# A fused two-block transformer kernel: the mixed 512 and 256-column form for more chunks of its feed-forward stages

## The chip, the core and the metric

The kernel runs on one core of a Trainium2 chip. The metric is the device time of one execution in microseconds (us). Each instruction belongs to an engine with its own in-order queue: TensorE (PE, with its weight loads shown as PEld), VectorE (DVE), ScalarE (ACT), GpSimd (POOL) and SyncE (SP), which here issues nearly all DMAs. Engines wait for each other through counting semaphores.

## The reference, cut to what matters

Two transformer blocks are applied to x of 256 rows and 1024 columns in float32. Four feed-forward layers (D_FF = 2816) take most of the work; the kernel calls them F0, F1, F2, F3. Between them lie a mixing layer with two kinds of attention (M1) and one with a Fourier part and latent attention (M2).

```
def swiglu(x, w_gate, w_up, w_down):
    return (jax.nn.silu(x @ w_gate) * (x @ w_up)) @ w_down

def first_block(...):
    mods = (jax.nn.silu(c) @ w_ada[l] + b_ada[l]).reshape(B, N_MOD, D_MODEL)
    n = modulate(rmsnorm(h, g_pre[l, 0]), shift(0), scale(0))
    f = swiglu(n, w_ffn_gate[l, 0], w_ffn_up[l, 0], w_ffn_down[l, 0])     # F0
    h = h + 0.5 * gate(0) * rmsnorm(f, g_post[l, 0])
    ...                                                                  # M1, F1

def second_block(...):
    mod = c_act @ ada_w[l] + ada_b[l]
    x = x + 0.5 * g1[:, None, :] * swiglu_2(h, ...)                      # F2
    ...                                                                  # M2, F3
```

The products `silu(c) @ w_ada` and `c_act @ ada_w` (1024 by 9216 each) are not done as matmuls of the stages. They are spread as work of DVE over the feed-forward stages, most of it in F0.

## The kernel before

**Precision.** Every float32 matrix is split into a high part and a low part in the type fp32r: ACT copies the raw weights to `w_hi` (`split_hi`, L816) and DVE subtracts to get `w_lo` (`split_lo`, L1201). A product is then three matmuls: hi by hi, hi by lo and lo by hi.

**A feed-forward stage** is cut into 11 chunks (NC) of 256 columns of D_FF. For a chunk c, PE makes the gate and the up product (`gate_up_half`, first half and second half of the 1024 rows of the weights, one 1 MB slot of weights each), then ACT takes Silu of the gate part and DVE multiplies it by the up part into `h_act`. While that goes on, PE does the down product of chunk c - 1 (`downs`), which needs `hT_hi` (ACT) and `hT_lo` (DVE, L1294) of that chunk. So one pass of `body` on PE is: wait for the product of chunk c - 1 (`h_ready`), gate and up of c, down of c - 1. The pass of `body` on DVE that belongs to it has the split of the down weights, `hT_lo`, the conditioning updates `ada`, the split of the next chunk's first half of gate and up weights, the product, and the split of the second half.

**Two forms of the gate and up product.** In the narrow form (`col_group`, L1929, L1931, L1932) all three matmuls of a block of 128 outputs have 256 columns, 96 matmuls per chunk. Four blocks share two PSUM banks; the product is one Silu on ACT and one multiplication on DVE (L1317). In the mixed form the high weights meet the high and the low part of the input side by side in one matmul of 512 columns (L1948), and the low weights meet the high part in one of 256 (L1954), so a chunk has 32 of 512 columns and 32 of 256. Each block then fills a bank of its own (banks 0 to 3), and what stands in the right half of a bank has to be added to the left half. That is an ACT copy, a DVE addition (L1307), the Silu on ACT (L897), an ACT copy and a DVE addition (L1309), and then the multiplication (L1312). `wide(f, c)` says which chunks take the mixed form: before, chunks 2 to 9 of F1, F2 and F3, none of F0. Chunk 0 of each stage is computed in rows (t = 0 and 1 are the two halves of the 256 rows) in banks 0 and 1, and is turned by transposes (`row_transposes`) in bank 0.

**The conditioning updates.** `ada(f, half, j)` (L1280 for j = 0, L1283 otherwise) adds row block j of the conditioning weights, times silu(c), to an accumulator; j runs from 0 to 7, one per chunk, in chunks 1 to 8. Each has one buffer in `arena` for each half, so the load of block j waits for the update with block j - 1. In F0 both halves have 3072 columns (1.5 MB each), in F1 1024 and 3072, in F2 3072 and 2048, in F3 1024 and none.

**What sets the order.** Each engine's order is written out by hand, with a hardware loop over the middle chunks. In `body` on DVE the place of the first update depends on the form:

```
if mods and wide(f, c):
    ada(f, 0, c - 1)
split_lo(*down_piece(f, c - 1))
...
if mods:
    if not wide(f, c):
        ada(f, 0, c - 1)
```

SP issues for each chunk, in this order: the down weights, the two conditioning loads, the two halves of the gate and up weights; each waits for the buffer that it fills.

Of the kernel before, what the change touches and what calls it, by code (L numbers as in the profile page):

```python
# [9 lines left out]
ALU = mybir.AluOpType  # L10
# [35 lines left out]
def program(nc, a, out):  # L46

    ctx = ExitStack()
    with ctx:
# [384 lines left out]

        def wide(f, c):

            return f != "F0" and (not isinstance(c, int) or 1 < c < NC - 1)

        def wide_at(f, c):

            return c + ((NC - 3) * (FFN.index(f) - 1) - 1)

        def down_piece(f, c):
            if isinstance(c, int) and c == NC - 1:
# [370 lines left out]
        def _(act):  # L815
# [63 lines left out]
            def body(f, c, extra=None):  # L879

                i = FFN.index(f) * NC
                split_hi(*down_piece(f, c - 1))
                if isinstance(c, int) and c == 1:
                    act.wait_ge(row_tr, FFN.index(f) + 1)
                    copy(hT_hi[:].rearrange("p j n -> p (j n)"), ps[:, 0, :]).then_inc(ht_hi, 1)
                else:
                    act.wait_ge(h_ready, c + i)
                    copy(hT_hi[:], h_act[:]).then_inc(ht_hi, 1)
                if extra:
                    split_hi(*extra)  # L890
                split_hi(*(down_piece(f, c) if isinstance(c, int) and c == NC - 1 else gate_up(f, 0, c + 1)))
                if wide(f, c):
                    act.wait_ge(gate_mm, wide_at(f, c))
                    act.wait_ge(h_ready, c + i)
                    copy(sil[:], ps[:, 0:2, S:2 * S]).then_inc(g_rest, 1)
                    act.wait_ge(g_sum, wide_at(f, c))
                    act.activation(sil[:], sil[:], ACT.Silu).then_inc(silu_done, 1)  # L897
                    used(act, gate_up(f, 1, c))
                    act.wait_ge(ht_lo, c + h_parts(f))
                    copy(h_act[:], ps[:, 2:4, S:2 * S]).then_inc(u_rest, 1)  # L900
                else:
                    used(act, gate_up(f, 1, c))
                    wait(act, h_ready, c + i)
                    b = 2 if isinstance(c, int) and c == 1 else 0
                    act.activation(sil[:], ps[:, b, :].rearrange("p (k n) -> p k n", n=S), ACT.Silu).then_inc(silu_done, 1)
                if not (isinstance(c, int) and c == NC - 1):
                    split_hi(*gate_up(f, 1, c + 1))

            def row_silu_out(f):

                i = FFN.index(f)
                act.wait_ge(row_mm, STAGES.index(f) + 1)
                act.activation(sil[:, 0, :], ps[:, 0, 0:FC], ACT.Silu).then_inc(row_silu, 1)
                used(act, gate_up(f, 1, 0))
                act.activation(sil[:, 1, :], ps[:, 1, 0:FC], ACT.Silu).then_inc(silu_done, 1)

            def ffn(f, next_e=None, next_b=None, n=PIECE):

# [3 lines left out]
                body(f, 1)  # L922
                if f == "F0":
                    used(act, down_piece(f, 0))
                with act.Fori(2, NC - 1) as c:
                    body(f, c)
                body(f, NC - 1, extra=next_e and (*next_e, n))
                act.wait_ge(h_ready, NC * (FFN.index(f) + 1))
# [261 lines left out]
        def _(dve):  # L1190
# [95 lines left out]
            def body(f, c, mods=False, hook=None, extra=None):  # L1286
# [3 lines left out]
                    ada(f, 0, c - 1)  # L1290
                split_lo(*down_piece(f, c - 1))
                dve.wait_ge(ht_hi, c + h_parts(f))
                h = ps[:, 0, :].rearrange("p (j n) -> p j n", n=S) if isinstance(c, int) and c == 1 else h_act[:]
                dve.tensor_tensor(hT_lo[:], h, hT_hi[:].bitcast(F32), ALU.subtract).then_inc(ht_lo, 1)  # L1294
                if mods:
                    if not wide(f, c):
# [579 lines left out]
        def _(pe):  # L1876
# [89 lines left out]
            def body(f, c, mid=None, first=None):  # L1966
                i = FFN.index(f) * NC
                if not (isinstance(c, int) and c <= 1):
                    pe.wait_ge(h_ready, c + i)
                if first:  # L1970
                    first()
                gate_up_half(f, 0, c)
                if mid:
                    mid()
                gate_up_half(f, 1, c)
                if isinstance(c, int) and c == NC - 1:
                    return
                downs(f, c)
# [590 lines left out]
```

## Time and profile before

| | |
|---|---|
| time, median of 3 runs | 1097.07 us (1097.07 to 1097.42) |
| profiled execution, its own time | 1097.06 us |
| its span in the trace | 1095.3 us |
| PE busy | 1066.7 us, 97% of the span |
| DVE busy | 848.7 us, 77% |
| ACT busy | 546.6 us, 50% |
| POOL busy | 50.3 us, 5% |
| chain that ended last | PE 88%, DVE 4%, ACT 2%, DMA 2% |

The span is that of the instructions of the traced execution; the time of the execution is 1.8 us longer. The chain that ended last is followed back from the last instruction, at each step to what released it. Busy shares are means over the whole kernel, and the stages differ: what a change is worth in one stage has to be read from the rows of that stage.

### The profile page before, as it was taken

The numbers are of one execution on the slowest core, as the hardware profiler recorded it, in microseconds if no ns is written. First come the engines' busy times: TensorE is split into PE (matmuls) and PEld (weight loads), VectorE is DVE, ScalarE is ACT, GpSimd is POOL, SyncE is SP. The second block draws the span as 40 slices with busy tenths as digits, with TensorE's granted clock in tenths as the row PEclk, the third lists the DMA queues.
The fourth block names the chain that finished last, engine by engine and source line by source line (L and its number), as shares of the span: only waits on it lengthen the run. The fifth ranks groups of instructions, "written<-read, shape, count | busy, mean of one in ns | idle before, by whom it ended". The sixth has DMA issues, their size and how long they took to land.

```text
span 1095.3 us, 16473 instructions
## 1 busy us (share of the span) xinstructions
PE 1066.7 (97%) x6295; PEld 939.1 (86%) x6295; DVE 848.7 (77%) x908; ACT 546.6 (50%) x658; POOL 50.3 (5%) x78
## 2 busy tenths in 40 slices
PE   3999999999999999999999999999999999999997
PEld 2999999889988788888988888898888878888886
DVE  6899888678887788888778998867875787666665
ACT  4444343564765644544564444455645356444452
POOL 1000000101221100000010000000100000000001
PEclk9999999999999999999999999999999999999999
DMA  9999997557424598997569999744562546766651
GB/s 340 381 402 390 388 396 262 171 118 230 134 78 154 192 337 312 321 313 239 187 243 383 344 352 355 250 145 135 185 223 78 175 133 216 229 213 232 220 177 58
DMA packets 147141, 265.28 MB, mean 242 GB/s; under 512 B 9769, under 2 KB 104470, under 8 KB 141974
## 3 DMA queue, kind: packets, MB, share of 16 engines
q1 hardware_dynamic: 145376, 261.30, 69.0%
q0 software_dynamic: 1056, 3.17, 1.0%
q8 instruction: 31, 0.51, 0.2%
q10 hardware_dynamic: 662, 0.16, 0.1%
q14 instruction: 16, 0.13, 0.0%
HBM read 263.34 MB, written 1.27 MB: 242 GB/s over the span
## 4 chain that ended last, share of the span: by engine, by line
PE 88%; DVE 4%; ACT 2%; DMA 2%; issue 2%; SPq 1%; POOL 1%; POOLq 0%; DVEq 0%; ACTq 0%
PE ps L1948 16%; PE ps L1879 12%; PE ps L1880 12%; PE ps L1881 12%; PE ps L1954 8%; PE ps L1929 7%; PE ps L1932 7%; PE ps L1931 7%; DMA w_raw<-in_w_ffn_up 1%; DMA arena<-in_w_ada 1%; ACT w_hi L816 1%; DVE w_lo L1201 1%; DVE y_row L1362 1%; SPq L631 1%; PE ps L1899 1%
## 5 line engine op out<-in xcount | busy, mean ns | idle before, releaser
L1201 DVE TENSOR_TENSOR w_lo<-w_raw,w_hi 128x2048 fp32r<-128x2048 f32 (+2 forms) x169 | 380.4, 2255 | 110.0 <-ACT w_hi L816 109.1
L816 ACT ACTIVATE w_hi<-w_raw 128x2048 fp32r<-128x2048 f32 (+2 forms) x169 | 317.5, 1883 | 261.1 <-PE ps L1881 112.1
L1929 PE MATMUL ps<-nT_both,w_hi 128*128 128x256 f32 x672 | 191.7, 285 | 0.0
L1932 PE MATMUL ps<-nT_both,w_lo 128*128 128x256 f32 x672 | 190.1, 283 | 0.0
L1931 PE MATMUL ps<-nT_both,w_hi 128*128 128x256 f32 x672 | 190.1, 283 | 0.0
L1948 PE MATMUL ps<-nT_both,w_hi 128*128 128x512 f32 x768 | 187.1, 391 | 0.0
L1948 PEld LDWEIGHTS ps<-nT_both,w_hi 128*128 128x128 f32 x768 | 141.1, 188 | 27.3
L1929 PEld LDWEIGHTS ps<-nT_both,w_hi 128*128 128x128 f32 x672 | 128.8, 192 | 0.9
L1283 DVE SCALAR_TENSOR_TENSOR arena<-arena,c_act 128x3072 f32<-128x3072 f32 (+2 forms) x49 | 129.4, 2650 | 0.0
L1931 PEld LDWEIGHTS ps<-nT_both,w_hi 128*128 128x128 f32 x672 | 128.9, 192 | 0.5
L1932 PEld LDWEIGHTS ps<-nT_both,w_lo 128*128 128x128 f32 x672 | 128.8, 192 | 0.0
L1879 PE MATMUL ps<-w_hi,hT_hi 128*128 128x512 f32 x320 | 125.0, 391 | 0.0
L1880 PE MATMUL ps<-w_lo,hT_hi 128*128 128x512 f32 x320 | 125.0, 391 | 0.0
L1881 PE MATMUL ps<-w_hi,hT_lo 128*128 128x512 f32 x320 | 124.5, 389 | 0.0
L1954 PEld LDWEIGHTS ps<-nT_both,w_lo 128*128 128x128 f32 x768 | 101.6, 191 | 5.6
L1954 PE MATMUL ps<-nT_both,w_lo 128*128 128x256 f32 x768 | 103.4, 282 | 0.0
L1879 PE MATMUL ps<-w_hi,nT_both 128*128 128x512 f32 (+2 forms) x256 | 99.9, 390 | 0.5 <-DVE nT_both L1221 0.3
L1881 PE MATMUL ps<-w_hi,nT_both 128*128 128x512 f32 (+2 forms) x256 | 97.5, 381 | 0.0
L1880 PE MATMUL ps<-w_lo,nT_both 128*128 128x512 f32 (+2 forms) x256 | 97.4, 380 | 0.0
L1881 PEld LDWEIGHTS ps<-w_hi,hT_lo 128*128 128x128 f32 x320 | 60.1, 188 | 12.8
L1879 PEld LDWEIGHTS ps<-w_hi,hT_hi 128*128 128x128 f32 x320 | 60.2, 188 | 11.5
L1880 PEld LDWEIGHTS ps<-w_lo,hT_hi 128*128 128x128 f32 x320 | 60.2, 188 | 11.0
(299 smaller groups left out, 1218.7 us busy)
## 6 DMA issues: line engine op xcount, KB each, us to landing
arena<-in_w_ada SPq DMA_DIRECT2D x16, 1536.0 KB, 9.5
arena<-in_ada_w SPq DMA_DIRECT2D x16, 1536.0 KB, 8.3
w_raw<-in_w_in SPq DMA_DIRECT2D x44, 512.0 KB, 4.6
w_raw<-in_ffn_w_down SPq DMA_DIRECT2D x44, 512.0 KB, 4.1
w_raw<-in_w_ffn_gate SPq DMA_DIRECT2D x42, 512.0 KB, 7.0
w_raw<-in_w_ffn_up SPq DMA_DIRECT2D x42, 512.0 KB, 8.2
w_raw<-in_w_ffn_down SPq DMA_DIRECT2D x42, 512.0 KB, 4.7
w_raw<-in_ffn_w_gate SPq DMA_DIRECT2D x42, 512.0 KB, 4.1
```

The lines of the kernel that those rows point to most:

```text
L631: sp.dma_start(dst, cols).then_inc(first_loaded[j], 16)
L816: copy = lambda o, i: act.activation(o, i, ACT.Copy)
L1201: dve.tensor_tensor(lo(s, n), raw(s, n), hi(s, n).bitcast(F32), ALU.subtract).then_inc(lo_ready[s], 1)
L1283: dve.scalar_tensor_tensor(acc, ada_raw[:, half, 0:n], c_act[:, blk, bass.ds(j, 1)], acc, ALU.mult, ALU.add)\
L1879: pe.matmul(o, xh, wh, start=start, stop=False, skip_group_check=True)
L1880: pe.matmul(o, xh, wl, start=False, stop=False, skip_group_check=True)
L1881: return pe.matmul(o, xl, wh, start=False, stop=stop, skip_group_check=True)
L1929: pe.matmul(o, hi(s)[:, cols], nT_hi[:, kk, :], start=(half == first_half and k == 0 and i % 2 == 0), stop=False, skip_group_check=True)
L1931: pe.matmul(o, hi(s)[:, cols], nT_lo[:, kk, :], start=False, stop=False, skip_group_check=True)
L1932: last = pe.matmul(o, lo(s)[:, cols], nT_hi[:, kk, :], start=False, stop=(half != first_half and k == 3), skip_group_check=True)
L1948: pe.matmul(ps[:, i, :], hi(s)[:, cols], nT_both[:, 4 * half + k].rearrange("p a n -> p (a n)"), start=(half == 0 and k == 0), stop=False, ...
L1954: last = pe.matmul(ps[:, i, 0:S], lo(s)[:, cols], nT_hi[:, kk, :], start=False, stop=(kk == KD - 1), skip_group_check=True)
```

## The change

The mixed form is given to chunks 3 to 9 of F0 and to chunk 1 of F1, F2 and F3. Since mixed chunk 1 fills banks 0 to 3, the second row tile of chunk 0 moves from bank 1 to bank 6 in these stages and the transposes from bank 0 to bank 7, and PE waits ahead of chunk 1 until DVE has read bank 0 (a second count on `row_silu`). In F0 the loops of ACT and PE begin at chunk 3, with chunk 2 written out ahead of them. The condition in DVE's `body` is not edited, but `wide` now answers otherwise.

```
         def wide(f, c):
-            return f != "F0" and (not isinstance(c, int) or 1 < c < NC - 1)
+            return not isinstance(c, int) or (2 if f == "F0" else 0) < c < NC - 1
+        def row_bank(f, t):
+            return t if f in ("F0", "M1", "M2") else 6 * t
+        def turned_bank(f):
+            return 0 if f == "F0" else 7
         def wide_at(f, c):
-            return c + ((NC - 3) * (FFN.index(f) - 1) - 1)
+            return c - 2 if f == "F0" else c + ((NC - 2) * FFN.index(f) - 2)
...
# ACT, body of chunk 1, and row_silu_out
-                    copy(hT_hi[:].rearrange("p j n -> p (j n)"), ps[:, 0, :]).then_inc(ht_hi, 1)
+                    copy(hT_hi[:].rearrange("p j n -> p (j n)"), ps[:, turned_bank(f), :]).then_inc(ht_hi, 1)
-                act.activation(sil[:, 1, :], ps[:, 1, 0:FC], ACT.Silu).then_inc(silu_done, 1)
+                act.activation(sil[:, 1, :], ps[:, row_bank(f, 1), 0:FC], ACT.Silu).then_inc(silu_done, 1)
...
# ACT, ffn; PE's ffn is changed in the same way, with NC - 2 as the end of its loop
-                with act.Fori(2, NC - 1) as c:
+                if f == "F0":
+                    body(f, 2)
+                with act.Fori(3 if f == "F0" else 2, NC - 1) as c:
...
# DVE, row_h
-                dve.wait_ge(row_silu, i + 1)
-                dve.tensor_tensor(h_act[:, 0, :], ps[:, 0, FC:2 * FC], sil[:, 0, :], ALU.mult)
+                dve.wait_ge(row_silu, 2 * i + 1)
+                dve.tensor_tensor(h_act[:, 0, :], ps[:, 0, FC:2 * FC], sil[:, 0, :], ALU.mult).then_inc(row_silu, 1)
...
# PE, body and ffn
                 if not (isinstance(c, int) and c <= 1):
                     pe.wait_ge(h_ready, c + i)
+                elif wide(f, c):
+                    pe.wait_ge(row_silu, 2 * FFN.index(f) + 2)
-                    first_rows(f, [gate_up(f, half, 0) for half in range(2)], NB, (0, 1))
+                    first_rows(f, [gate_up(f, half, 0) for half in range(2)], NB, [row_bank(f, t) for t in range(T)])
```

What this does to the order on DVE in the loop of F0 (chunks 3 to 8) follows. The names are those of the tiles: `w_lo<-w_raw,w_hi` is a split of weights, `arena<-arena,c_act` a conditioning update, `hT_lo` the low part of the turned product, `h_act` the product; hi_ready2 is the slot of the down weights, hi_ready0 and hi_ready1 the two halves of gate and up. Lines are those of each kernel. Before:

```order
L1201 TENSOR_TENSOR w_lo<-w_raw,w_hi 128x2048 [waits hi_ready2]
L1294 TENSOR_TENSOR hT_lo<-h_act,hT_hi 128x512 [waits ht_hi]
L1277 ISA
L1283 ISA [waits ada_done0,ada_loaded0]
L1283 SCALAR_TENSOR_TENSOR arena<-arena,c_act 128x3072
L1283 SCALAR_TENSOR_TENSOR arena<-arena,c_act 128x3072 [waits ada_done1,ada_loaded1]
L1200 REGISTER_ALU
L1201 TENSOR_TENSOR w_lo<-w_raw,w_hi 128x2048 [waits hi_ready0]
L1317 TENSOR_TENSOR h_act<-ps,sil 128x512 [waits ht_lo,silu_done]
L1201 TENSOR_TENSOR w_lo<-w_raw,w_hi 128x2048 [waits hi_ready1]
```

The same loop on DVE in the changed kernel:

```order
L1293 ISA [waits ada_done0,ada_loaded0]
L1293 SCALAR_TENSOR_TENSOR arena<-arena,c_act 128x3072
L1211 TENSOR_TENSOR w_lo<-w_raw,w_hi 128x2048 [waits hi_ready2]
L1304 TENSOR_TENSOR hT_lo<-h_act,hT_hi 128x512 [waits ht_hi]
L1293 SCALAR_TENSOR_TENSOR arena<-arena,c_act 128x3072 [waits ada_done1,ada_loaded1]
L1210 REGISTER_ALU
L1211 TENSOR_TENSOR w_lo<-w_raw,w_hi 128x2048 [waits hi_ready0]
L1316 REGISTER_ALU
L1317 TENSOR_TENSOR sil<-ps,sil 128x512 [waits g_rest]
L1319 TENSOR_TENSOR h_act<-ps,h_act 128x512 [waits u_rest]
L1322 TENSOR_TENSOR h_act<-h_act,sil 128x512 [waits u_sum,silu_done]
L1211 TENSOR_TENSOR w_lo<-w_raw,w_hi 128x2048 [waits hi_ready1]
```

The first conditioning update, with its wait for its load, has moved from behind the split of the down weights and `hT_lo` to the head of the pass, and two additions that wait for ACT stand ahead of the multiplication.

On PE, this is where chunk 0 of F1 ends (rows of L1879 to L1881, L1889 to L1891 in the changed kernel) and the first half of chunk 1 begins. Before:

```order
L1879 MATMUL ps<-w_hi,nT_both 128x512
L1880 MATMUL ps<-w_lo,nT_both 128x512
L1881 MATMUL ps<-w_hi,nT_both 128x512
L1929 MATMUL ps<-nT_both,w_hi 128x256 [waits lo_ready0]
L1931 MATMUL ps<-nT_both,w_hi 128x256
L1932 MATMUL ps<-nT_both,w_lo 128x256
```

In the changed kernel, up to the transposes of chunk 0:

```order
L1889 MATMUL ps<-w_hi,nT_both 128x512
L1890 MATMUL ps<-w_lo,nT_both 128x512
L1891 MATMUL ps<-w_hi,nT_both 128x512
L1958 MATMUL ps<-nT_both,w_hi 128x512 [waits lo_ready0,row_silu]
L1958 MATMUL ps<-nT_both,w_hi 128x512 x15
L1964 MATMUL ps<-nT_both,w_lo 128x256 x16
L2074 MATMUL ps<-ident,h_act 128x128 [waits h_ready]
```

The first matmul of chunk 1 now also waits for DVE's first product of chunk 0, and 16 matmuls of 512 and 16 of 256 columns stand where 48 of 256 stood.

## Rows read from the trace of the kernel before

**Rows 1.** Windows of PE chunks; columns: stretch, length, busy of each engine, clock, DMA.
```profile
93.80:178.70 84.90, 84.90 (x602) 80.11 (x601) 73.31 (x36) 33.88 (x25) 0.00 (x0) 1.00 0.97 361
178.70:195.68 16.98, 16.98 (x122) 16.02 (x121) 11.46 (x8) 6.75 (x5) 0.00 (x0) 1.00 0.82 285
...
601.73:684.70 82.97, 82.97 (x441) 71.70 (x440) 74.38 (x46) 39.97 (x35) 0.00 (x0) 1.00 0.97 351
378.98:390.93 11.95, 11.95 (x102) 11.95 (x101) 9.85 (x7) 6.39 (x5) 0.00 (x0) 1.00 0.79 264
25.29:28.42 3.13, 3.13 (x8) 2.45 (x9) 2.72 (x5) 3.06 (x6) 0.00 (x0) 1.00 1.07 377
```

**Rows 2.** The page's second part: DMA share in 40 slices, in tenths.
```profile
DMA  9999997557424598997569999744562546766651
```

**Rows 3.** Timeline of DVE in F0, chunk 3: start, length, instruction, idle before.
```profile
76.11 2.29 DVE L1201 TENSOR_TENSOR w_lo<-w_raw,w_hi 128x2048 fp32r<-128x2048 f32 x1
79.03 2.29 DVE L1201 TENSOR_TENSOR w_lo<-w_raw,w_hi 128x2048 fp32r<-128x2048 f32 x1 [0.63 <-ACT w_hi L816]
81.23 0.69 DVE L1294 TENSOR_TENSOR hT_lo<-h_act,hT_hi 128x512 fp32r<-128x512 f32 x1
81.84 3.42 DVE L1283 SCALAR_TENSOR_TENSOR arena<-arena,c_act 128x3072 f32<-128x3072 f32 x1
...
89.05 2.29 DVE L1201 TENSOR_TENSOR w_lo<-w_raw,w_hi 128x2048 fp32r<-128x2048 f32 x1 [0.47 <-ACT w_hi L816]
91.25 0.69 DVE L1317 TENSOR_TENSOR h_act<-ps,sil 128x512 f32<-128x512 f32 x1
```

**Rows 4.** Conditioning loads of chunks 3 and 4: issue, then time to landing.
```profile
L571 SPq DMA_DIRECT2D arena<-in_w_ada x1: 333/333/333, 69.1 to 69.1; - x1
DMA to landing us min/median/max: 11.3/11.3/11.3
...
L571 SPq DMA_DIRECT2D arena<-in_w_ada x1: 333/333/333, 85.5 to 85.5; - x1
DMA to landing us min/median/max: 10.8/10.8/10.8
```

**Rows 5.** Timeline of DVE in F2, one whole pass in the mixed form.
```profile
644.98 0.68 DVE L1307 TENSOR_TENSOR sil<-ps,sil 128x512 f32<-128x512 f32 x1
646.96 0.69 DVE L1309 TENSOR_TENSOR h_act<-ps,h_act 128x512 f32<-128x512 f32 x1 [1.30 <-ACT h_act L816]
647.75 0.69 DVE L1312 TENSOR_TENSOR h_act<-h_act,sil 128x512 f32<-128x512 f32 x1
648.76 2.29 DVE L1201 TENSOR_TENSOR w_lo<-w_raw,w_hi 128x2048 fp32r<-128x2048 f32 x1 [0.32 <-ACT w_hi L816]
650.97 3.41 DVE L1283 SCALAR_TENSOR_TENSOR arena<-arena,c_act 128x3072 f32<-128x3072 f32 x1
654.30 2.29 DVE L1201 TENSOR_TENSOR w_lo<-w_raw,w_hi 128x2048 fp32r<-128x2048 f32 x1
656.50 0.69 DVE L1294 TENSOR_TENSOR hT_lo<-h_act,hT_hi 128x512 fp32r<-128x512 f32 x1
657.10 2.35 DVE L1283 SCALAR_TENSOR_TENSOR arena<-arena,c_act 128x2048 f32<-128x2048 f32 x1
659.37 2.28 DVE L1201 TENSOR_TENSOR w_lo<-w_raw,w_hi 128x2048 fp32r<-128x2048 f32 x1
661.57 0.68 DVE L1307 TENSOR_TENSOR sil<-ps,sil 128x512 f32<-128x512 f32 x1
```

**Rows 6.** Timeline of DVE in F1: the two additions of chunk 2.
```profile
406.95 0.68 DVE L1307 TENSOR_TENSOR sil<-ps,sil 128x512 f32<-128x512 f32 x1
408.81 0.69 DVE L1309 TENSOR_TENSOR h_act<-ps,h_act 128x512 f32<-128x512 f32 x1 [1.18 <-ACT h_act L816]
```

**Rows 7.** Timelines of DVE and of PE's weight loads where F1's chunk 1 begins.
```profile
378.39 0.42 DVE L1329 TENSOR_TENSOR h_act<-ps,sil 128x256 f32<-128x256 f32 x1
...
378.76 0.19 PEld L1929 LDWEIGHTS ps<-nT_both,w_hi 128*128 128x128 f32 x1
```

More of the change, by code:

```diff
@@ L1292, in body @@
                 dve.wait_ge(ht_hi, c + h_parts(f))
-                h = ps[:, 0, :].rearrange("p (j n) -> p j n", n=S) if isinstance(c, int) and c == 1 else h_act[:]
+                h = ps[:, turned_bank(f), :].rearrange("p (j n) -> p j n", n=S) if isinstance(c, int) and c == 1 else h_act[:]
                 dve.tensor_tensor(hT_lo[:], h, hT_hi[:].bitcast(F32), ALU.subtract).then_inc(ht_lo, 1)
@@ L1327, in row_h @@
                 wait(dve, ht_lo, h_parts(f))
-                dve.wait_ge(row_silu, i + 1)
-                dve.tensor_tensor(h_act[:, 0, :], ps[:, 0, FC:2 * FC], sil[:, 0, :], ALU.mult)
+                dve.wait_ge(row_silu, 2 * i + 1)
+                dve.tensor_tensor(h_act[:, 0, :], ps[:, 0, FC:2 * FC], sil[:, 0, :], ALU.mult).then_inc(row_silu, 1)
                 dve.wait_ge(silu_done, NC * i + 1)
-                dve.tensor_tensor(h_act[:, 1, :], ps[:, 1, FC:2 * FC], sil[:, 1, :], ALU.mult).then_inc(h_ready, 1)
+                dve.tensor_tensor(h_act[:, 1, :], ps[:, row_bank(f, 1), FC:2 * FC], sil[:, 1, :], ALU.mult).then_inc(h_ready, 1)
             def ffn(f, next_e=None):
@@ L2061, in row_transposes @@
                     for t in range(T):
-                        last = pe.transpose(ps[:, 0, j * S + t * P:j * S + (t + 1) * P], h_act[:, t, j * P:(j + 1) * P], ident[:])
+                        last = pe.transpose(ps[:, turned_bank(f), j * S + t * P:j * S + (t + 1) * P], h_act[:, t, j * P:(j + 1) * P], ident[:])
                 last.then_inc(row_tr, 1)
@@ L2124, in ffn @@
                 else:
-                    first_rows(f, [gate_up(f, half, 0) for half in range(2)], NB, (0, 1))
+                    first_rows(f, [gate_up(f, half, 0) for half in range(2)], NB, [row_bank(f, t) for t in range(T)])
                     body(f, 1, mid=lambda: row_transposes(f))
-                with pe.Fori(2, NC - 2) as c:
+                if f == "F0":
+                    body(f, 2)
+                with pe.Fori(3 if f == "F0" else 2, NC - 2) as c:
                     body(f, c)
```

## The prediction

> **What bounds the kernel now.** I read three views: windows laid over PE's chunks, then DVE's timeline in the same chunks, then the landing times of the loads. In the windows [rows 1] a chunk is one pass of PE, from the first matmul of gate and up to the end of the down product. PE is busy in every microsecond of them, and chunks follow each other at a fixed pace. In F0 chunk 4 begins at 93.80, chunk 9 at 178.70 and chunk 10 at 195.68: five chunks in 84.90 us, 16.98 each, in the narrow form. F2, in the mixed form, takes 82.97 us for five, 16.594 each. So PE bounds both stages, and the mixed form is worth 16.98 - 16.594 = 0.386 us per chunk on PE.
>
> The other engines are nearer to PE than the page's shares say. DVE's pass in F2 [rows 5] is to be read from one first addition (644.98) to the next (661.57), 16.59 us, PE's own pace. Inside it the only idle times are 1.30 and 0.32 us, and both come from its own first addition: Silu and a copy on ACT have to follow it before the second addition, and the split of the high part stands behind that copy on ACT. Nothing in the pass waits for PE except, perhaps, that copy. So the mixed form with updates of 3072 and 2048 columns fits under PE with next to no room. In F0 both updates have 3072. F0's DMA share is 0.97 in its chunks [rows 1], 9 in the page's first slices [rows 2], so landing times count there as well.
>
> **Term 1, PE's own work.** Ten chunks turn mixed (seven in F0, three times chunk 1): 10 x 0.386 = 3.9 us less, if PE never waits. The saving is what 32 matmuls fewer per chunk cost beside equal columns: 96 of 256 against 32 of 512 and 32 of 256.
>
> A rule of the Trainium skill speaks against this term. "TensorE: Matmul & The Clock Gate", section "Back-to-back issue gap", gives a warm gap of N / 2.4 + 2.5 ns for isolated matmuls. By it 32 fewer would save 32 x 2.5 ns = 0.08 us per chunk, an estimate from that page, and the ten chunks 0.8 us. The windows show 0.386 in this kernel, so the measurement decides. By the page the three chunks of term 4 would bring 0.2 instead of 1.2 us, and the whole sum would end about 0.9 us higher than mine, since in F0 PE's pace will not matter.
>
> **Term 2, the first mixed chunk of F0.** DVE is strictly in order, and its first instruction in chunk 3 is now the update, which waits for its load. That load is issued at 69.1 and lands 11.3 us later, at 80.4 [rows 4]. All before that is untouched by the change, so this time stands. Before, it did no harm: DVE split the down weights at 79.03, did `hT_lo` at 81.23 and came to the update at 81.84 [rows 3]. Now DVE ends the split of 76.11 at about 78.4 and stands until 80.4. From there, with distances from start to start [rows 5]: update 3.33 (650.97 to 654.30), split 2.20, `hT_lo` 0.60, second update 3.33 (also 3072 columns), split 2.20 gives the first addition at 92.06. The second follows 1.98 later, the product 0.79 after it, and it ends 0.69 after that, at 95.5. Before, the product started at 91.25 and ended at 91.9 [rows 3]. PE wants it for chunk 4, which began at 93.80 and would now begin at 93.80 - 0.39 = 93.4. It begins at 95.6 with some 0.1 us for the signal. PE waits 2.2 us. The second split of that pass needs weights that landed before 89.05 in the old order too, so no load ends later than this chain.
>
> **Term 3, DVE's pace in F0.** From here the cover is gone: PE stands at the product, and DVE sets the pace. Its pass is that of F2 [rows 5] with 3.33 in place of 2.27 (657.10 to 659.37) for the second update: 16.59 + 1.06 = 17.65 us. The copy on ACT may have waited in F2 for the end of PE's up product; in F1 the two additions stand 408.81 - 406.95 = 1.86 apart [rows 6], so it can give back 0.12, or 17.53. I take 17.57, with 17.5 and 17.65 as bounds. Loads are no bound at that pace: the next first update is loaded by 85.5 + 10.8 = 96.3 [rows 4], and DVE comes to it at 95.5 + 0.3 + 2.2 = 98.0. The products of chunks 4 to 8 follow at this distance, so chunk 9 begins at 95.6 + 5 x 17.57 = 183.5 (17.65 would give 183.9, 17.5 gives 183.1). Chunk 9 has no updates, DVE has room in it, and PE takes its 16.6: chunk 10 begins at 200.1 instead of 195.68 [rows 1]. F0 costs **+4.4 us** (4.0 to 4.9), in which PE's 7 x 0.386 of gain is already counted. Behind F0 there is a chain over PE, ACT and DVE that starts from the last products, and all shifts by the same time.
>
> **Term 4, chunk 1 of F1, F2 and F3.** It takes 11.95 us without the down product in the narrow form, the transposes in its middle included [rows 1], and should take 0.39 less. The new wait: DVE's first product of chunk 0 ends at 378.39 + 0.42 = 378.81, and PE's weight load for chunk 1 began at 378.76 [rows 7]. So PE is held 0.05 to 0.15 us. What stands behind the waiting matmul is all of chunk 1, and nothing else waits there. Three times (0.39 - 0.10) gives **-0.9 us**. Later on DVE in these stages: in steady F2 the product ends at 647.75 + 0.69 = 648.44, and PE begins its next chunk at 651.51 (601.73 + 3 x 16.594), a cover of 3.07 us. With chunk 1 mixed, DVE's passes start up to 1.9 us later by my estimate (the two additions and ACT's part between them, less idle time that DVE had there), which leaves 1.2 us. If that cover were gone, each 0.1 us short would be paid once, at the worst some 0.7 us in F2.
>
> Moving rows and transposes to banks 6 and 7 costs nothing: the same instructions on the same engines. The down product that fills these banks waits for `hT_lo` as before, which reads bank 7. Chunk 2 of F0 written out is the same work.
>
> **Sum:** +4.4 - 0.9 = +3.5 us. The profiled execution took 1097.06 us, its span 1095.3; the median of the runs is 1097.07. So 1100.6 us, 0.3% slower. A change within 0.2% (2.2 us) is about what a measurement of this kernel cannot tell from none.
>
> **Rivals.**
> - *The gain arrives* (0.09): DVE keeps up with PE in F0. For it: F2 carries the mixed form with updates of 5120 columns at no loss, and DVE is busy only 73.31 of 84.90 us in F0 [rows 1]. Then the time is 1097.1 - 3.9 + 0.3 = 1093.5, faster. It decides at a DVE pass of 16.59 us in F0, which needs 1 us less than the rows give, and at the first load, which would have to land 2 us earlier.
> - *A wash* (0.09): the waits on ACT inside DVE's pass shrink when PE is not ahead, and the pass is about 17.1. Then F0 costs 4.4 - 5 x 0.5 = 1.9, and the time is 1098.1.
> - *The loads join in* (0.07): the first update ahead of the down split delays the release of the down slot by some 5 us in chunk 3 (79.03 + 2.3 before, 86.0 now), SP stands there in order, and behind it are four more loads of a queue that is full [rows 1, 2]. If each of five chunks lost another 0.5 us, the time is 1103.1. Against it: DVE's new pace asks for fewer bytes per us than the queue moves now.
> - *TensorE slows* (0.05): the wait of 2.2 us in chunk 4 and about 1 us in each chunk after it leave matmuls slower. At 25.29 the first eight 512-column matmuls of F0 took 3.13 us [rows 1], 0.39 each against 0.23 later, though the granted clock reads 1.00, the level of 2.4 GHz, there. Once, that is 8 x 0.16 = 1.3 us, partly hidden since DVE sets the pace: 1101.5.
>
> **How the numbers follow.** The main case has 0.70 and its own range is 1099.9 to 1101.4: 0.9 between the bounds of term 3 and some tenths in term 4. The range for 8 in 10 takes in the slowing of TensorE, part of the loads' case and the slower end of the wash: 1098.3 to 1102.6. Slower by over 0.2%: 0.70 + 0.07 + 0.05 = 0.82, faster 0.08, the same 0.10, which holds most of the wash.
>
> **What would show it.** In the profile of the changed kernel: DVE idle for about 2 us until about 80.4 ahead of the first update of F0's chunk 3, released by a DMA; PE's first idle time of about 2.2 us ahead of chunk 4, released by DVE's product; chunks 4 to 8 of F0 17.6 us apart with about 1 us of PE idle in each; chunk 10 at 200.1. In F1 to F3 no idle time on PE but 0.1 us ahead of chunk 1, and chunks still 16.59 apart. I am wrong if DVE's pass in F0 is not 17.6, if the wait at chunk 3 is for something else, or if PE shows a wait at chunk 3 of F2.

## The result: 1100.34 us, 0.3% slower

The changed kernel takes 1100.34 us (median of 8 runs, 1099.93 to 1100.86), the kernel before on the same chip 1097.07 (8 runs, 1096.91 to 1097.42). The ratio is 1.0030 with a 95% interval of 1.0021 to 1.0039. The prediction was 1100.6, in a range from 1098.3 to 1102.6. The profiled execution has a span of 1098.5 us, 3.2 more than before.

Windows over PE's chunks in the changed kernel. The columns are as in [rows 1]: stretch, length, busy time of PE, PEld, DVE, ACT, POOL, then the granted clock, DMA share and GB/s. The windows are F0's chunks 4 to 8, F0's chunk 9, five chunks of F2, and F1's chunk 1.

```profile
95.72:183.45 87.73, 85.75 (x441) 72.55 (x441) 79.72 (x45) 38.56 (x36) 0.00 (x0) 0.98 0.96 342
183.45:200.18 16.73, 16.73 (x89) 14.45 (x90) 14.87 (x11) 7.98 (x8) 0.00 (x0) 1.00 0.78 282
605.32:688.29 82.97, 82.97 (x442) 71.71 (x441) 74.94 (x46) 39.29 (x35) 0.00 (x0) 1.00 0.97 349
383.30:394.89 11.59, 11.59 (x69) 10.27 (x69) 9.59 (x7) 6.99 (x6) 0.00 (x0) 1.00 0.80 260
```

The number of matmuls fell as meant: 441 in five chunks of F0 where it was 602. The time of these chunks did not: 87.73 us against 84.90, so 17.55 each instead of 16.98. PE is busy 85.75 of 87.73 us here, and in every other window all the time. F2's five chunks are unchanged at 82.97. F1's chunk 1 is 0.36 us shorter. In the order of [rows 1], chunk 4 begins 1.92 later than before (95.72 against 93.80), chunk 9 4.75 later (183.45, 178.70), and chunk 10 4.50 later (200.18, 195.68), because chunk 9 (16.73 against 16.98) is the only one of them that gives something back.

What PE waited for ahead of the mixed gate and up products (L1958), over the whole run: engine, line and what it waited for, then us in total, times, longest.

```profile
PE ps L1958 <- DVE h_act L1322: 4.1, 4, 2.1
```

And waits of the other engines and of PE's weight loads, in 60 to 205 us:

```profile
ACT w_hi L824 <- DMA w_raw<-in_w_ffn_up: 32.3, 7, 7.8
...
DVE h_act L1319 <- ACT h_act L824: 8.3, 7, 1.2
...
PEld ps L1958 <- DVE h_act L1322: 6.2, 5, 2.6
...
DVE arena L1293 <- DMA arena<-in_w_ada: 2.1, 1, 2.1
```

Line 1322 is DVE's product that gates the next chunk's gate and up. All of PE's waits for it lie in F0: 2.13 us ahead of chunk 4, and 0.66, 0.65 and 0.66 ahead of chunks 7, 8 and 9. A wait of 0.66 goes with a chunk of 17.55 us, 0.94 over PE's own 16.6. Of the rest, 0.16 is in the records' ends, since a matmul counts 0.39 us while the next one follows 0.23 behind it, and 0.13 is in the first 16 matmuls behind the wait, which take 3.76 us from start to start (148.36 to 152.12) where they take 3.63 without a wait (114.06 to 117.69); no run shows why. DVE itself waited for one load, once, 2.1 us, and seven times 1.2 us for ACT's copy between its two additions. That is its only large idle time in a steady pass. It lies directly ahead of the product on which PE stands (144.94 + 0.68 to 146.81, the product ends at 148.30, PE goes on at 148.36), so it delays PE although PE is still busy with its down product while DVE idles. ACT's 32.3 us of waiting for weights do not reach DVE in a steady pass: the split at 107.65 follows the update of 104.32 without a gap.

DVE's timeline in chunk 3 and in the pass that follows (start, length, instruction, idle before), to be set beside [rows 3] and [rows 5]:

```profile
76.26 2.29 DVE L1211 TENSOR_TENSOR w_lo<-w_raw,w_hi 128x2048 fp32r<-128x2048 f32 x1
80.64 3.42 DVE L1293 SCALAR_TENSOR_TENSOR arena<-arena,c_act 128x3072 f32<-128x3072 f32 x1 [2.08 <-DMA arena<-in_w_ada]
83.97 2.29 DVE L1211 TENSOR_TENSOR w_lo<-w_raw,w_hi 128x2048 fp32r<-128x2048 f32 x1
86.17 0.69 DVE L1304 TENSOR_TENSOR hT_lo<-h_act,hT_hi 128x512 fp32r<-128x512 f32 x1
86.78 3.41 DVE L1293 SCALAR_TENSOR_TENSOR arena<-arena,c_act 128x3072 f32<-128x3072 f32 x1
90.11 2.29 DVE L1211 TENSOR_TENSOR w_lo<-w_raw,w_hi 128x2048 fp32r<-128x2048 f32 x1
92.31 0.68 DVE L1317 TENSOR_TENSOR sil<-ps,sil 128x512 f32<-128x512 f32 x1
94.17 0.69 DVE L1319 TENSOR_TENSOR h_act<-ps,h_act 128x512 f32<-128x512 f32 x1 [1.18 <-ACT h_act L824]
94.97 0.69 DVE L1322 TENSOR_TENSOR h_act<-h_act,sil 128x512 f32<-128x512 f32 x1
95.97 2.29 DVE L1211 TENSOR_TENSOR w_lo<-w_raw,w_hi 128x2048 fp32r<-128x2048 f32 x1 [0.31 <-ACT w_hi L824]
...
109.85 0.68 DVE L1317 TENSOR_TENSOR sil<-ps,sil 128x512 f32<-128x512 f32 x1
```

The first row with an idle time is the one to find: the update of 80.64 waited 2.08 us for its load. All rows behind it run without a gap until ACT's 1.18. The product ends at 94.97 + 0.69 = 95.66, and PE begins chunk 4 at 95.72. The next first addition is at 109.85, 17.54 us after that of 92.31: DVE's pass, and the pace of PE.

Chunk 1 of F1, at its start, in the timelines of DVE, PE's weight loads and PE, answers to [rows 7]:

```profile
382.70 0.42 DVE L1339 TENSOR_TENSOR h_act<-ps,sil 128x256 f32<-128x256 f32 x1
...
382.85 0.19 PEld L1891 LDWEIGHTS ps<-w_hi,nT_both 128*128 128x128 f32 x1
383.18 0.54 PEld L1958 LDWEIGHTS ps<-nT_both,w_hi 128*128 128x128 f32 x3
...
383.07 0.39 PE L1891 MATMUL ps<-w_hi,nT_both 128*128 128x512 f32 x1
383.30 0.85 PE L1958 MATMUL ps<-nT_both,w_hi 128*128 128x512 f32 x3
```

The product ends at 383.12 and the weight load begins at 383.18, 0.33 after the load ahead of it. But the matmul of 383.07 is still streaming, and the next one follows it at 383.30, 0.23 later, the usual distance. The new wait is there, on the weight load, and it costs nothing here.

Ahead of chunks 5 and 6 PE shows no wait, and this needs the windows of chunks 4 and 5 apart, and of the first 16 matmuls of each:

```profile
95.72:114.06 18.34, 18.34 (x88) 15.60 (x89) 16.48 (x10) 7.99 (x8) 0.00 (x0) 0.91 0.98 352
114.06:130.81 16.75, 16.75 (x90) 14.16 (x88) 15.41 (x9) 7.65 (x7) 0.00 (x0) 1.00 1.00 354
95.72:101.11 5.39, 5.39 (x17) 4.28 (x17) 5.14 (x2) 2.54 (x3) 0.00 (x0) 0.68 1.02 380
114.06:117.69 3.63, 3.63 (x18) 3.00 (x16) 3.63 (x2) 2.44 (x2) 0.00 (x0) 1.00 0.97 385
```

Chunk 4 took PE 18.34 us of unbroken work, at a granted clock of 0.91 behind the wait of 2.13 us: part of it ran at the lower level, 1.2 GHz. That part lies in the first 16 matmuls, which took 5.39 us at 0.68, against 3.63 at 1.00 in chunk 5. Chunk 4 cost 18.34 - 16.6 = 1.7 us more than PE's own pace. DVE's product was ready at 112.51 + 0.69 = 113.20, and PE came to it only at 114.06. In chunk 5 PE caught up, and chunk 6 began at 130.81, when the next product was ready (130.06 + 0.69 = 130.75). So the slow matmuls fitted into the 0.94 us per chunk that DVE leaves over, and chunk 6 began where it would have begun anyway.

### The profile page after: what moved, and what is told of

It is laid out like the page before. It is cut to its first block, busy times and chain, and to the rows that moved or that the text cites. A ratio compares the mean times of both kernels' runs of the same rounds, so it can differ in the third digit from the quotient of the medians.

```text
span 1098.5 us, 15893 instructions
## 1 busy us (share of the span) xinstructions
PE 1065.7 (97%) x5975; PEld 922.8 (84%) x5975; DVE 862.1 (78%) x928; ACT 555.8 (51%) x678; POOL 50.4 (5%) x78
## 4 chain that ended last, share of the span: by engine, by line
PE 77%; DVE 8%; issue 6%; ACT 4%; DMA 3%; SPq 1%; POOL 1%; DVEq 0%; ACTq 0%; POOLq 0%
PE ps L1958 19%; PE ps L1889 11%; PE ps L1890 11%; PE ps L1891 11%; PE ps L1964 10%; PE ps L1939 3%; PE ps L1942 3%; PE ps L1941 3%; DVE w_lo L1211 3%; DMA arena<-in_w_ada 2%; ACT w_hi L824 2%; DMA w_raw<-in_w_ffn_up 1%; DVE arena L1293 1%; DVE y_row L1372 1%; PE ps L1909 1%
## 5 line engine op out<-in xcount | busy, mean ns | idle before, releaser
L1958 PE MATMUL ps<-nT_both,w_hi 128*128 128x512 f32 x1088 | 267.6, 393 | 4.1 <-DVE h_act L1322 4.1
L1958 PEld LDWEIGHTS ps<-nT_both,w_hi 128*128 128x128 f32 x1088 | 200.6, 189 | 45.3 <-DVE h_act L1322 6.2
L1964 PEld LDWEIGHTS ps<-nT_both,w_lo 128*128 128x128 f32 x1088 | 143.9, 191 | 8.0
L1964 PE MATMUL ps<-nT_both,w_lo 128*128 128x256 f32 x1088 | 146.4, 282 | 0.0
L1889 PE MATMUL ps<-w_hi,hT_hi 128*128 128x512 f32 x320 | 125.0, 391 | 0.0
L1891 PE MATMUL ps<-w_hi,hT_lo 128*128 128x512 f32 x320 | 124.5, 389 | 0.0
L1939 PE MATMUL ps<-nT_both,w_hi 128*128 128x256 f32 x352 | 100.9, 287 | 0.0
L1889 PE MATMUL ps<-w_hi,nT_both 128*128 128x512 f32 (+2 forms) x256 | 99.8, 390 | 0.5 <-DVE nT_both L1231 0.3
L1941 PE MATMUL ps<-nT_both,w_hi 128*128 128x256 f32 x352 | 99.6, 283 | 0.0
L1942 PE MATMUL ps<-nT_both,w_lo 128*128 128x256 f32 x352 | 99.5, 283 | 0.0
L1891 PE MATMUL ps<-w_hi,nT_both 128*128 128x512 f32 (+2 forms) x256 | 97.6, 381 | 0.0
L1891 PEld LDWEIGHTS ps<-w_hi,hT_lo 128*128 128x128 f32 x320 | 60.1, 188 | 12.8
L905 ACT ACTIVATE sil<-sil 128x512 f32<-128x512 f32 x34 | 21.5, 632 | 95.6 <-DVE sil L1317 95.6
L1889 PEld LDWEIGHTS ps<-w_hi,hT_hi 128*128 128x128 f32 x320 | 60.2, 188 | 11.5
L1939 PEld LDWEIGHTS ps<-nT_both,w_hi 128*128 128x128 f32 x352 | 67.4, 192 | 0.5
L1941 PEld LDWEIGHTS ps<-nT_both,w_hi 128*128 128x128 f32 x352 | 67.5, 192 | 0.1
```

The costliest lines, as they stand in the source:

```text
L1889: pe.matmul(o, xh, wh, start=start, stop=False, skip_group_check=True)
L1891: return pe.matmul(o, xl, wh, start=False, stop=stop, skip_group_check=True)
L1939: pe.matmul(o, hi(s)[:, cols], nT_hi[:, kk, :], start=(half == first_half and k == 0 and i % 2 == 0), stop=False, skip_group_check=True)
L1941: pe.matmul(o, hi(s)[:, cols], nT_lo[:, kk, :], start=False, stop=False, skip_group_check=True)
L1942: last = pe.matmul(o, lo(s)[:, cols], nT_hi[:, kk, :], start=False, stop=(half != first_half and k == 3), skip_group_check=True)
L1958: pe.matmul(ps[:, i, :], hi(s)[:, cols], nT_both[:, 4 * half + k].rearrange("p a n -> p (a n)"), start=(half == 0 and k == 0), stop=False, ...
```

## The experiments

Two theories were open. **T1**, mine: DVE's own work bounds F0 in the mixed form (the first wait from a load and an update placed early, then a pass of 17.55 us). **T2**: the loads bound it (the DMA share is 0.96, and the down slot comes free later). Beside them stood the question whether the parts add up, and whether the mixed form can be had in F0 at all.

### The two parts alone

`e1_chunk1_only` keeps chunk 1 of the later stages mixed and gives F0 back its narrow form:

```
-            return not isinstance(c, int) or (2 if f == "F0" else 0) < c < NC - 1
+            return f != "F0" and (not isinstance(c, int) or 0 < c < NC - 1)
```

> The change without its part in F0: F0 stays narrow throughout, chunk 1 of F1, F2 and F3 is mixed. Main theory (the three chunks bring a gain, all of the loss is F0's): each chunk 1 takes 11.6 us instead of 11.95, so 1097.1 - 1.1 = 1096.0 us. Rival (the moved banks and the new wait eat the gain, or part of the loss sits in F1 to F3): 1097.1 us or more.

Measured: 1096.02 us, ratio 0.9989 (0.9979 to 0.9998). F0's chunks are back at 16.98. The three chunks gain 1.0 us by the times, near the 1.1 of the windows.

`e2_f0_only` is the other half, with chunk 1 narrow and F0 as in the change:

```
-            return not isinstance(c, int) or (2 if f == "F0" else 0) < c < NC - 1
+            return not isinstance(c, int) or (2 if f == "F0" else 1) < c < NC - 1
```

> The change without mixed chunk 1: chunks 3 to 9 of F0 mixed, chunk 1 of F1, F2 and F3 narrow (chunk 0's rows stay in banks 6 and 7). Main theory: F0's loss stands alone, chunk 10 of F0 begins at 200.2, 1097.1 + 4.5 = 1101.5 us. Rival (a part of F0's loss is given back or grows behind it, through the loads of M1 or the moved banks): anything but the sum of the two parts, 1101.5.

Measured: 1101.45 us, 1.0039 (1.0023 to 1.0054). Against the kernels before of their own runs the halves are -1.0 and +4.3 us, in sum 3.3. The whole change is 3.3. They add up: the loss comes with F0's mixed chunks, and chunk 1 gains.

### Work of DVE or bytes of the load

Both kernels touch only the second conditioning part of F0's loop, where 3072 columns are loaded and updated. `e3_short_update` computes 2048 of them and still loads all:

```
                     dve.wait_ge(ada_done[half], j + n_ada[f])
+                    if f == "F0" and half and not isinstance(j, int):
+                        n, acc = 2 * D, mod_acc[:, half, 0:2 * D]
```

> The changed kernel, but from chunk 3 of F0 on the second conditioning update computes 2048 of its 3072 columns on DVE (1024 columns of the conditioning sums miss these row blocks; the loads are all there). Main theory (DVE's pass of 17.55 us sets F0's pace): the pass falls to 16.5, PE is the bound again at 16.59 per chunk, chunk 4 begins at 94.7 and chunk 10 at 194.3 instead of 200.2, so 1100.3 - 5.9 = 1094.4 us. Rival (the loads of F0 set the pace, since the queue is full): nothing changes in the loads, so chunks stay 17.5 us apart and the time is 1099 to 1100.3. Rival (mixed matmuls are slower in F0 on PE itself): 1100.3.

`e4_short_load` loads 2048 of them and still computes on all:

```
                 settle(j)
+                if f == "F0" and half and not isinstance(j, int):
+                    n = 2 * D
```

> The changed kernel, but from chunk 3 of F0 on the second conditioning load brings 2048 of 3072 columns (0.5 MB less per chunk; DVE computes all columns, on stale values in 1024 of them). Main theory (DVE's pass sets the pace, loads land early): no change, chunks 17.55 apart, chunk 10 at 200.2, 1100.3 us. Rival (loads set the pace): 0.5 MB at about 400 GB/s is 1.3 us less per chunk, the pace falls to PE's 16.59 and the time to about 1095.5 us.

Measured: e3 1094.63 us, 0.9979 (0.9969 to 0.9990); e4 1100.25 us, 1.0029 (1.0018 to 1.0041). The windows over F0's chunks 4 to 8, first of e3:

```profile
94.68:177.80 83.12, 83.12 (x441) 71.81 (x441) 74.84 (x46) 38.92 (x36) 0.00 (x0) 1.00 1.01 371
```

and of e4:

```profile
95.55:183.27 87.72, 84.48 (x440) 71.33 (x440) 79.72 (x45) 38.81 (x36) 0.00 (x0) 1.00 0.90 316
```

One us less of DVE's work per pass, and PE is back at 16.62 us per chunk, with the DMA share at 1.01 and 371 GB/s, more than in the changed kernel. A sixth less of conditioning loads, which is a twelfth less of all bytes (316 GB/s x 17.54 us = 5.5 MB per chunk, against 342 x 17.55 = 6.0), and nothing moves: 17.54 per chunk. This settles T1 against T2 for the steady pace. The first wait is another matter. It is for the load of the first half, which e4 leaves as it was, and it is still there:

```profile
80.47 3.42 DVE L1295 SCALAR_TENSOR_TENSOR arena<-arena,c_act 128x3072 f32<-128x3072 f32 x1 [1.83 <-DMA arena<-in_w_ada]
```

### The first wait

`e5_old_place` puts F0's first update back behind `hT_lo`, as in the kernel before; the later stages keep it ahead of the down split:

```
-                if mods and wide(f, c):
+                if mods and wide(f, c) and f != "F0":
                     ada(f, 0, c - 1)
...
-                    if not wide(f, c):
+                    if not wide(f, c) or f == "F0":
                         ada(f, 0, c - 1)
```

> The changed kernel with the first conditioning update of F0 back behind the split of the down weights and hT_lo. Main theory: DVE no longer stands at the load in chunk 3, but its split of the next gate and up weights then waits for their load until 89.05, so the product comes only 1.1 us earlier (chunk 4 at 94.7); the pass is as long as before, 17.55 per chunk, chunk 10 at 199.1, 1099.3 us. Rival (the place of the update is the cause of the whole loss): 1096 us or less, chunks 16.6 apart.

Measured: 1099.53 us, 1.0021 (1.0011 to 1.0030). No row of DVE waits for a load in chunk 3 now. Its product starts at 94.20 instead of 94.97, and PE begins chunk 4 at 94.95 after 0.90 us of waiting. The pace behind it is unchanged (112.49, 130.03, 147.57, 165.12, 182.66, so 17.54 each). So the early place of the update is worth 0.8 us, once, and the rest of the loss is the pass. (Profiled executions differ by some tenths before anything of the change is reached: chunk 3 begins at 77.29 here and at 76.83 in the changed kernel. So 0.8 holds to a few tenths; the medians of the times also differ by 0.8.)

### Filling the idle time between the additions

The pass has 1.18 us of idle time in which an update could lie. `e6_fill` puts the first update behind `hT_lo` and the second between the two additions, in F0:

```
+                fill = mods and wide(f, c) and f == "F0"
...
                     dve.tensor_tensor(sil[:], ps[:, 0:2, 0:S], sil[:], ALU.add).then_inc(g_sum, 1)
+                    if fill:
+                        ada(f, 1, c - 1)
```

> The changed kernel with DVE's order in F0 rearranged: the first conditioning update behind hT_lo, and the second one between the two additions, where DVE stood idle for Silu and copy on ACT. Same work in all. Main theory (DVE's pass, idle time inside it included, sets the pace): the pass loses 1.2 us of idle time ahead of the second addition and falls to about 16.7, chunks 4 to 8 of F0 are 16.7 apart; chunk 3 is worse, since the product waits for the split at 89.05 and then for an update, so chunk 4 begins at 96.7 and chunk 10 at 197.0, 1097.1 us. Rival (only DVE's busy time counts, not the wait on ACT): no change from 1100.3, or 1099.3 as with the old place.

Measured: 1102.2 us, 1.0049 (1.0033 to 1.0064), slower than the changed kernel and 5.1 us over the forecast. Nothing was wrong with the idle time: it is gone. SP's queue shows where it went (start, length, instruction):

```profile
123.92 7.20 SPq L579 DMA_DIRECT2D arena<-in_w_ada  x2
131.38 0.38 SPq L561 DMA_DIRECT2D w_raw<-in_w_ffn_gate  x1
131.85 0.46 SPq L561 DMA_DIRECT2D w_raw<-in_w_ffn_up  x1
```

Then ACT, and DVE behind it:

```profile
140.00 1.92 ACT L824 ACTIVATE w_hi<-w_raw 128x2048 fp32r<-128x2048 f32 x1 [5.46 <-DMA w_raw<-in_w_ffn_up]
...
136.87 3.41 DVE L1293 SCALAR_TENSOR_TENSOR arena<-arena,c_act 128x3072 f32<-128x3072 f32 x1
141.95 2.29 DVE L1211 TENSOR_TENSOR w_lo<-w_raw,w_hi 128x2048 fp32r<-128x2048 f32 x1 [1.67 <-ACT w_hi L824]
144.16 0.68 DVE L1318 TENSOR_TENSOR sil<-ps,sil 128x512 f32<-128x512 f32 x1
144.76 3.41 DVE L1293 SCALAR_TENSOR_TENSOR arena<-arena,c_act 128x3072 f32<-128x3072 f32 x1
148.08 0.68 DVE L1322 TENSOR_TENSOR h_act<-ps,h_act 128x512 f32<-128x512 f32 x1
```

The slot of the second conditioning load comes free only when the late update before it has ended, at 130.5. The first row holds both conditioning issues, at 123.9 and 130.8, so SP stands between them. Behind it in order stand gate's and up's weights, which have a free slot and get out at 131.38 and 131.85. In the changed kernel this gate load was issued at 127.72, 3.1 us ahead of chunk 6; here it is 0.6 ahead (132.00). The two land 7.1 and 8.1 us after their issue, at 138.5 and 140.0. The new order also asks for them sooner, since the second update no longer stands ahead of their split: DVE is ready for it at 136.87 + 3.41 = 140.28, 8.3 us into chunk 6, where the changed kernel comes to it at 142.74, 11.9 us into the chunk. ACT waits 5.46 us for the weights and DVE 1.67 for ACT. The pass has won 1.18 and lost it again through another engine's queue: chunks 6 to 9 begin at 132.00, 149.62, 167.19 and 184.59, still 17.5 apart. The first wait is also longer here, 3.22 us ahead of chunk 4 at 96.89.

`e9_fill_loads` is e6 with one more edit, on SP: in F0 the first half of the next gate and up weights is issued ahead of the second conditioning load.

```
                     load_ada(f, 0, c - 1)
+                    if f == "F0":
+                        load_gu(f, 0, c + 1)
+                        load_ada(f, 1, c - 1)
+                    else:
+                        load_ada(f, 1, c - 1)
+                        load_gu(f, 0, c + 1)
```

> The rearranged DVE order in F0 (second update between the two additions), and SP issues the first half of the next gate and up weights ahead of the second conditioning load in F0's loop. Reading of the rearranged order alone: its passes stayed 17.5 us apart because the late second update held SP, and the weights behind it, so that the idle time only moved to the split of these weights. If so, with this issue order the split finds its weights, passes fall to PE's 16.59 in all of F0, chunk 3's product is in time as well, chunk 10 begins at about 193.0, and the time is 1097.1 - 2.7 - 1.1 = 1093.3 us. Rival (the queue itself cannot bring the bytes of a mixed chunk in 16.6 us): passes of 17 us or more, 1095.5 us or more.

Measured: **1093.14 us, 0.9964 (0.9950 to 0.9978)**, faster than both kernels. F0's chunks 4 to 8 in the windows of e9:

```profile
93.37:176.41 83.04, 83.04 (x441) 71.75 (x441) 79.73 (x46) 39.54 (x35) 0.00 (x0) 1.00 1.02 378
```

SP's queue in e9:

```profile
120.91 0.38 SPq L561 DMA_DIRECT2D w_raw<-in_w_ffn_gate  x1
121.39 0.46 SPq L561 DMA_DIRECT2D w_raw<-in_w_ffn_up  x1
124.83 0.35 SPq L579 DMA_DIRECT2D arena<-in_w_ada  x1
```

And a pass of DVE in e9:

```profile
128.84 2.29 DVE L1215 TENSOR_TENSOR w_lo<-w_raw,w_hi 128x2048 fp32r<-128x2048 f32 x1 [0.64 <-ACT w_hi L828]
131.05 0.68 DVE L1309 TENSOR_TENSOR hT_lo<-h_act,hT_hi 128x512 fp32r<-128x512 f32 x1
131.66 3.41 DVE L1297 SCALAR_TENSOR_TENSOR arena<-arena,c_act 128x3072 f32<-128x3072 f32 x1
134.99 2.28 DVE L1215 TENSOR_TENSOR w_lo<-w_raw,w_hi 128x2048 fp32r<-128x2048 f32 x1
137.19 0.68 DVE L1322 TENSOR_TENSOR sil<-ps,sil 128x512 f32<-128x512 f32 x1
137.79 3.41 DVE L1297 SCALAR_TENSOR_TENSOR arena<-arena,c_act 128x3072 f32<-128x3072 f32 x1
141.11 0.68 DVE L1326 TENSOR_TENSOR h_act<-ps,h_act 128x512 f32<-128x512 f32 x1
```

DVE does the same 79.73 us of work as in the changed kernel (79.72), in 83.04 instead of 87.73. The additions touch the update between them on both sides, PE has no wait from chunk 3 to the end of F0, and its pace is 16.61. In chunk 3 the split of the next gate and up weights starts at 85.63 instead of 89.05 ([rows 3]), and the product ends at 93.24, 0.13 us before PE needs it.

`e10_loads_only` is the changed kernel with SP's edit alone, so that it is known which of the two edits did it.

> The changed kernel with its own DVE order, and only the issue order of SP changed in F0's loop (first half of the next gate and up weights ahead of the second conditioning load). Main theory (DVE's pass with its idle time for ACT sets the pace at 17.55, loads are early in it): no gain, chunks 17.55 apart, the time 1100.3 to 1100.9 us, since the second update of chunk 3 may wait some tenths for its later load. Rival (the issue order alone is what helped): 1097 us or less.

Measured: 1100.66 us, 1.0033 (1.0020 to 1.0046). Against the changed kernel (1100.34), the new order of loads alone brings nothing (+0.3), the new order of DVE alone (e6) loses 1.9, and both together gain 7.2; against the kernel before they stand at +3.5, +5.0 and -4.1. So SP's order is shown as what kept e6's pass at 17.5, and not only read from its trace.

### Fewer mixed chunks

`e7_from_7` has the mixed form in F0's chunks 7, 8 and 9 only (written out, beside chunk 1 of the later stages), so that DVE's lag has two passes to build up:

```
+            if f == "F0":
+                return isinstance(c, int) and 7 <= c < NC - 1
```

> Mixed form in F0 for chunks 7, 8 and 9 alone, chunk 1 of F1 to F3 mixed as in the change. Main theory: two chunks with updates at 17.55 instead of 16.98 only use up the cover that DVE's product has ahead of PE there (about 2.3 us), PE never waits, and each mixed chunk brings 0.39: chunk 10 begins at 194.5 instead of 195.7, 1097.1 - 1.2 - 1.1 = 1094.8 us, faster than both kernels. Rival (mixed chunks with two updates of 3072 columns always lose): 1097 us or more.

Measured: 1094.82 us, 0.9979 (0.9970 to 0.9988). PE never waits for the product. Its chunks 7 and 8 take 16.60 and 16.59 us, though DVE's pass was 17.5 in the changed kernel: the narrow chunks ahead leave DVE room. The product ends 2.41 us before PE needs it ahead of chunk 7 (142.71 and 145.12), 1.11 ahead of chunk 8 and 0.15 ahead of chunk 9 (178.16 and 178.31). The forecast's two passes would have used up 1.9 of this; a wait of 0.69 us for a conditioning load at 145.59 took some more, and the kernel got through with 0.15 left. Chunk 9 has no updates. Chunk 10 began at 194.94 and not at 194.5, since this execution was 0.4 us late at chunk 3 already (77.20 against 76.81).

`e8_from_6_fill` goes one further: mixed from chunk 6, with the update between the additions in chunks 7 and 8, and SP's order as it was.

> Mixed form in F0 for chunks 6 to 9, with the second update of chunks 7 and 8 between the two additions, chunk 1 of F1 to F3 mixed. Main theory: the cover is used up over one chunk, the filled passes then keep PE's pace, chunk 10 begins at 194.1, 1097.1 - 1.5 - 1.1 = 1094.5 us, a few tenths under the kernel with chunks 7 to 9. Rival: the later product makes PE wait in chunks 8 and 9, and the time is 1095 us or more.

Measured: 1095.69 us, 0.9987 (0.9978 to 0.9996), over the forecast and on the side of its rival. PE waits in chunk 9:

```profile
178.23 2.14 PE L1967 MATMUL ps<-nT_both,w_hi 128*128 128x512 f32 x8 [0.36 <-DVE h_act L1329]
```

and ACT waited before it, as in e6:

```profile
168.60 1.92 ACT L826 ACTIVATE w_hi<-w_raw 128x2048 fp32r<-128x2048 f32 x1 [4.80 <-DMA w_raw<-in_w_ffn_up]
```

The cover was 0.80 us ahead of chunk 7 and 0.37 ahead of chunk 8, and then it was gone. Chunk 10 began at 195.00 where 194.1 was forecast. Of these 0.9 us, 0.52 are in chunk 8 (17.12 us with the wait at its end) and 0.17 in chunk 9 (16.77), and 0.17 were there at chunk 3 (76.98 against 76.81). The median of the times lies 0.3 above the profiled execution (1095.40).

## Why the prediction was right, step by step

**What bounds the kernel.** The reading that DVE, next in line behind PE, would set the pace was right. DVE had next to no room under PE's mixed pace in F2 with updates of 5120 columns, and none with 6144. e3 shows the border from one side (5120 in F0: 16.62 per chunk), the change from the other (17.55). The total, +3.3 us against +3.5, is the sum of small misses of both signs, given below.

**Term 1.** The mixed form saves 0.36 to 0.38 us in each chunk 1 (11.59 against 11.95 in F1, 11.57 against 11.94 and 11.95 in F2 and F3), near the 0.386 taken from the windows. In F0 the saving is visible where DVE allows it: e9's chunks take 16.61 against 16.98. The formula in "TensorE: Matmul & The Clock Gate" of the Trainium skill, section "Back-to-back issue gap", would have given 0.08 per chunk (an estimate from that page). The section gives it for an isolated matmul and says itself that streams of weight loads and matmuls keep other distances; no window here agrees with 0.08, and the measurement decides.

**Term 2, the first wait.** Forecast: load in at 80.4, PE waits 2.2 us, chunk 4 at 95.6. Measured: 80.6, 2.1 and 95.72. e5 prices the place of the update in it at 0.8 us, e3 the longer second update at 1.0 (94.68 against 95.72).

**Term 3, DVE's pace.** Forecast 17.57 per pass, measured 17.55, and the reason given for taking less than 17.65 was the right one: the distance of the additions shrank to 94.17 - 92.31 = 1.86. Chunk 9 was forecast at 183.5 and came at 183.45; chunk 10 at 200.1 and came at 200.18. F2 of the changed kernel confirms the sum: once DVE runs late there, its pass is 16.48 us (product to product, 603.71 to 620.19, shown below), and 16.48 + 1.06 = 17.54. One of the signs to look for was put too high: about 1 us of PE idle in each of the chunks was forecast, and the profile shows 0.66 ahead of chunks 7, 8 and 9 and none ahead of 5 and 6, for the reasons given with the result. Chunk 9 took 16.73 instead of 16.6, the 0.13 behind a wait. F0 lost 4.50 against the forecast +4.4.

**Term 4** was the one with a size off: -0.9 forecast, -1.1 measured in the windows, and -1.0 by e1's time. The wait of 0.1 us falls on the weight load, and the matmul ahead of it covers it. The late cover held, but was thinner than the 1.2 us estimated. In F2 of the changed kernel:

```profile
603.71 0.69 DVE L1322 TENSOR_TENSOR h_act<-h_act,sil 128x512 f32<-128x512 f32 x1
...
620.19 0.69 DVE L1322 TENSOR_TENSOR h_act<-h_act,sil 128x512 f32<-128x512 f32 x1
```

The first product ends at 604.40 and PE begins its next chunk at 605.32, 0.92 us later, where it was 3.1 before; after that the cover grows by about 0.1 per chunk. PE never waited for the product in F1 to F3, so the case of 0.7 us in F2 did not occur.

The span rose by 3.2, not by 4.5 - 1.1 = 3.4: F1's chunk 1 begins 4.32 later than before, so some 0.2 us came back between F0's end and there. It came back in M1, at one DVE instruction of the attention. The same instruction before and in the changed kernel:

```profile
317.39 0.74 DVE L1616 TENSOR_REDUCE stat<-arena 128x1 f32<-128x128 f32 x2 [0.53 <-DVE arena L1610]
...
321.60 0.74 DVE L1626 TENSOR_REDUCE stat<-arena 128x1 f32<-128x128 f32 x2
```

It starts 4.21 later, and the instruction ahead of it on DVE 4.58 later (316.31, 320.89): the idle time of 0.53 us ahead of it is all but gone. e1 has it, e2 does not. Why it comes and goes is not shown. The prediction let everything behind F0 shift by the same time, so these 0.2 us lie outside its terms.

**The rivals.** *The gain arrives* would need what e9 does, another order on two engines; with it the time is 1093.14, near this rival's 1093.5. *A wash* supposed shorter waits on ACT; they shrank by 0.12, not by 0.5. *The loads join in* is refuted for this kernel by e4; e6 shows that the mechanism it spoke of, SP standing in order, is real as soon as a slot is released late enough. *TensorE slows* did happen, in one chunk: 1.7 us in chunk 4 at a granted clock of 0.91, more than the 1.3 forecast, but all of it lay under DVE's pace and chunk 6 was not late. I had called it partly hidden; it was hidden whole. e2 and e4, where PE waited 1.71 and 1.74 us and the clock stayed at 1.00, begin chunk 10 at 200.30 and 200.00, no earlier to speak of than the changed kernel's 200.18.

## What to carry to other kernels

A form that saves time on the busiest engine must be set against the next engine's pass, worked out from start to start in a stage that already runs in that form; here 3.33 us in place of 2.27 in one instruction turned a gain of 0.39 per chunk into a loss of 0.57. Idle time inside that pass is room only if what is moved into it releases nothing too late: look at which queue waits for the buffer that the moved instruction frees, and what else stands in that queue. And two edits that each bring nothing or a loss can be a gain together, so test the pair when the trace of the first names the second.

## What was not expected of the hardware

The length of a wait did not decide whether TensorE's clock fell. Behind 2.13 us (the changed kernel) and 3.22 us (e6) the chunk ran at 0.91 and took 18.34 and 18.36 us; behind 2.88 us in e10 the next 17.58 us read 1.00:

```profile
96.42:114.00 17.58, 16.93 (x89) 14.30 (x89) 15.94 (x9) 7.81 (x8) 0.00 (x0) 1.00 0.97 361
```

Three profiles do not tell what decides it, and no run was made for it.

A wait that falls on PE's weight load alone, 0.1 us at 383.18, leaves no mark on the matmuls, since the load runs under the matmul before it (0.39 us long in the records, the next one 0.23 behind).

The full queue was no limit on the steady pace. At 316 GB/s and a DMA share of 0.90 (e4) F0 was slow, at 378 GB/s and 1.02 (e9) it was fast. A share near 1 in a window was therefore no sign that the transfers came late. A single load can be late all the same: a conditioning load of 1.5 MB landed 11.3 us after its issue in [rows 4], and DVE stood for it in chunk 3 of the changed kernel; one of the same size landed 6.2 us after its issue in e6, where SP had stood before it.
